# Splitting the mixers' weight chunks in two halves of two row slices each

## The reference, cut to what matters

```python
def _token_mix(xc, xl, w_in, b_in, ...):
    seg_c = _split_proj(xc @ w_in + b_in)
    seg_l = _split_proj(xl @ w_in + b_in)
    ...
    return merge(...) @ w_out

def second_block(x, ...):
    for l in range(DEPTH_2):
        x = x + 0.5 * swiglu(rmsnorm(x, ffn1_norm[l]), ...)
        h = rmsnorm(x, mix_norm[l])
        proj = h @ w_in[l]
        ...
        y = gm[:, :, 0] * (o_a @ w_branch_nsa[l]) + gm[:, :, 1] * (o_b @ w_branch_gla[l])
        x = x + y @ w_out[l]
        x = x + 0.5 * swiglu(rmsnorm(x, ffn2_norm[l]), ...)
```

## Time and profile before

| | |
|---|---|
| median of 3 runs | 2517.67 us (2512.25 to 2520.01) |
| the profiled execution | 2515.03 us, its span 2513.3 us |
| TensorE busy | 2424.2 us, 96% |
| VectorE busy | 1422.5 us, 57% |
| ScalarE busy | 1151.6 us, 46% |
| `mix_split`, L1419 | 120 instructions, 227 us on ScalarE |
| `mix_low`, L2039 | 120 instructions, 272 us on VectorE |
| mean HBM traffic | 159 GB/s |

### The profile page before, as it was taken

One profiled execution on the slowest core, in us unless ns is written; L12 is line 12 of the kernel. 1 busy time (PEld: TensorE's weight loads), 2 busy tenths in 40 slices (PEclk: granted clock), 3 DMA queues, 4 the chain that ended last, 5 costly groups with the idle time before them and its releaser, 6 DMA issues.

```text
span 2513.3 us, 33003 instructions
## 1 busy us (share of the span) xinstructions
PE 2424.2 (96%) x13542; PEld 2007.6 (80%) x13542; DVE 1422.5 (57%) x2035; ACT 1151.6 (46%) x1602; POOL 15.3 (1%) x47
## 2 busy tenths in 40 slices
PE   6999999999999989998999999999999999999998
PEld 4777788888878777887888887788888888777887
DVE  3222233746655667666666467566666654756665
ACT  4211232534532335445444468554454445864444
POOL 0000000000000000000000000000000000000000
PEclk9999999999999999999999999999999999999999
DMA  8654222323521224554454733345545545335553
GB/s 320 237 224 178 97 88 100 134 78 124 188 82 66 85 84 150 194 184 167 169 186 183 256 138 145 118 168 190 195 168 184 191 183 189 126 111 176 184 185 133
DMA packets 57653, 399.64 MB, mean 159 GB/s; under 512 B 7785, under 2 KB 8305, under 8 KB 10016
## 3 DMA queue, kind: packets, MB, share of 16 engines
q1 hardware_dynamic: 52704, 383.80, 42.1%
q10 hardware_dynamic: 3688, 9.02, 1.0%
q0 software_dynamic: 1120, 4.78, 0.5%
HBM read 396.52 MB, written 2.63 MB: 159 GB/s over the span
## 4 chain that ended last, share of the span: by engine, by line
PE 90%; DVE 5%; ACT 3%; DMA 1%; issue 1%; POOL 0%; SPq 0%; ACTq 0%; DVEq 0%
PE pair L466 82%; DMA ring<-in_stream 1%; DVE ring_parts L2039 1%; PE pair L797 1%; PE pair L592 1%; DVE ring_parts L2031 1%; PE pair L1213 1%; ACT mix_high L1419 1%; PE pair L780 1%; PE pair L1185 1%; PE pair L934 1%; PE pair L575 1%; PE pair L1199 1%; PE pair L744 0%; ACT arena L1370 0%
## 5 line engine op out<-in xcount | busy, mean ns | idle before, releaser
L466 PE MATMUL pair<-xT_parts,ring_high 128*128 128x512 f32 x2112 | 745.7, 395 | 3.3 <-DVE xT_parts L2023 3.3
L466 PE MATMUL pair<-xT_parts,ring_parts 128*128 128x256 f32 (+2 forms) x2448 | 693.9, 298 | 14.4 <-DVE ring_parts L2039 12.1
L2031 DVE TENSOR_TENSOR ring_parts<-ring,ring_high 128x2048 fp32r<-128x2048 f32 x198 | 453.6, 2292 | 160.6 <-ACT ring_high L1407 160.5
L466 PEld LDWEIGHTS pair<-xT_parts,ring_parts 128*128 128x128 f32 (+1 forms) x2448 | 460.8, 188 | 63.3 <-issue 25.4
L466 PEld LDWEIGHTS pair<-xT_parts,ring_high 128*128 128x128 f32 x2112 | 383.9, 188 | 79.2 <-issue 4.0
L1407 ACT ACTIVATE ring_high<-ring 128x2048 fp32r<-128x2048 f32 x198 | 378.1, 1911 | 97.6 <-DMA ring<-in_stream 97.4
L1451 ACT ACTIVATE arena<-pair 128x512 f32<-128x512 f32 x110 | 66.0, 600 | 309.0 <-PE pair L466 309.0
L2039 DVE TENSOR_TENSOR ring_parts<-ring,mix_high 128x2048 fp32r<-128x2048 f32 x68 | 153.5, 2286 | 67.9 <-ACT mix_high L1419 67.9
L466 PE MATMUL pair<-ring_parts,xT_parts 128*128 128x512 f32 (+1 forms) x448 | 175.7, 392 | 0.9 <-DVE rows L2247 0.9
L466 PE MATMUL pair<-mix_high,xT_parts 128*128 128x512 f32 (+1 forms) x576 | 172.9, 383 | 0.0
L466 PE MATMUL pair<-ring_parts,g_high 128*128 128x512 f32 x440 | 171.4, 390 | 0.0
(11 more groups left out here) (368 smaller groups left out, 3896.3 us busy)
## 6 DMA issues: line engine op xcount, KB each, us to landing
ring<-in_stream SPq DMA_DIRECT2D x338, 1024.0 KB, 4.8
xn<-in_mods SPq DMA_DIRECT2D x14, 1024.0 KB, 6.6
arena<-in_mods SPq DMA_DIRECT2D x14, 1024.0 KB, 9.0
arena<-in_bT ACTq DMA_DIRECT2D x1, 1536.0 KB, 10.2
bias_scratch<-bias_row POOLq DMA_DIRECT2D x1, 1536.0 KB, 9.4
X<-in_x ACTq DMA_DIRECT2D x1, 1024.0 KB, 11.9
X<-in_ctx ACTq DMA_DIRECT2D x1, 1024.0 KB, 16.4
arena<-in_bT ACTq DMA_DIRECT2D x1, 1024.0 KB, 8.2
```

The lines of the kernel that those rows point to most:

```text
L466: m = pe.matmul(o, l, r, start=start, stop=stop)
L2031: dve.tensor_tensor(out=ring_r[:, slot].rearrange("p a b -> p (a b)"), in0=w, in1=high[:, slot, :], op=ALU.subtract).then_inc(low_ready, 1)
```

## The change

The high part of a mixer chunk is made by two ScalarE copies of two slices (1024 columns) each, and the low part by two VectorE subtractions of the same size. Both count their semaphores once per half. VectorE waits before each half for that half's high part, and TensorE asks at every second slice for the half that it starts on. The ffns' chunks are left as they were. Nothing changes its place in an engine's order; every row of a mixer's split becomes two, and TensorE gets 198 more rows with a wait on `mixer_low_parts` (198 before, 396 now).

```diff
             def mix_weights(k, cols, wait):
 
                 m, slot = c.mix + k // CW, (c.chunk + k // CW) % SLOTS
-                if wait and k % CW == 0:
-                    pe.wait_ge(mix_low_ready, split_before(len(mix_chunk) - 2, m + 1))
+                if wait and k % 2 == 0:
+                    pe.wait_ge(mix_low_ready, 2 * split_before(len(mix_chunk) - 2, m) + k % CW // 2 + 1)
...
-                act.activation(mix_high(l, m), ring[:, ch % SLOTS].rearrange("p a b -> p (a b)"),
-                               ACT.Copy).then_inc(mix_high_ready, 1)
+                for half in (slice(0, 2 * N), slice(2 * N, 4 * N)):
+                    act.activation(mix_high(l, m)[:, half], ring[:, ch % SLOTS].rearrange("p a b -> p (a b)")[:, half],
+                                   ACT.Copy).then_inc(mix_high_ready, 1)
...
                 slot = (mix_chunk[l + 1] + m) % SLOTS
-                dve.wait_ge(mix_high_ready, split_before(l, m + 1))
-                w = ring[:, slot].rearrange("p a b -> p (a b)")
-                dve.tensor_tensor(out=ring_r[:, slot].rearrange("p a b -> p (a b)"), in0=w, in1=mix_high(l, m),
-                                  op=ALU.subtract).then_inc(mix_low_ready, 1)
+                for n in range(2):
+                    half = slice(2 * n * N, 2 * (n + 1) * N)
+                    dve.wait_ge(mix_high_ready, 2 * split_before(l, m) + n + 1)
+                    w = ring[:, slot].rearrange("p a b -> p (a b)")[:, half]
+                    dve.tensor_tensor(out=ring_r[:, slot].rearrange("p a b -> p (a b)")[:, half], in0=w,
+                                      in1=mix_high(l, m)[:, half], op=ALU.subtract).then_inc(mix_low_ready, 1)
```

## The result

The changed kernel took 2504.4 us, the median of 7 runs (2498.7 to 2506.7), against 2515.1 us for the kernel before, the median of 7 (2512.3 to 2520.0). The ratio of the two is 0.9946, with a 95% interval of 0.9936 to 0.9956: 0.54% faster, 13.6 us by the ratio and 10.7 by the medians.

What follows compares the result with a forecast made beforehand. TensorE, with 90% of the chain, was taken as the bound. Terms 5.6 + 1.4 + 2.3 + 0.6 - 0.4 = 9.5 us gave 2505.5 from the profile, 2508.2 from the median; predicted 2507, range 2501 to 2516.

Steps and rivals of the forecast that it cites:

- the clock: Rival: TensorE's clock drops after idle time may vanish or appear; one is about 1.7 us either way; chance 0.15.
- Price of a half: Two halves instead of a whole chunk cost ScalarE 0.08 us and VectorE 0.02 us more per chunk.
- Term 1: The two layer mixers: shorter TensorE stalls at chunks 6, 10 and 11 gain 2.8 us per layer, 5.6 in all.
- Terms 2 to 4: Gains at the norms before the layer mixers, 1.4 us; in hgrn, 2.3 us; at the end of mlstm, 0.6 us.
- Term 5: TensorE's 198 more rows with a wait cost 0 to 0.8 us, taken as 0.4.
- The ring: Rival: full DMA engines keep chunk 10's transfer from coming sooner; 1.4 of 2.8 us stay per layer, 2511; chance 0.15.
- Nothing comes through: Rival: another wait follows each shortened TensorE stall; gain 0 to 3 us, time 2516; chance 0.15.
- the bare weight loads: Rival: added TensorE waits keep 188 ns weight loads from running ahead, costing 37 us; time 2544; chance 0.05.

Runs made afterwards that it cites:

- The two comparisons: The unaltered changed kernel timed twice against the kernel before: 2504.4 against 2515.1 us, ratio 0.9946; then 2502.0 against 2517.5, ratio 0.9933.
- The first-mixers version: Against the kernel before, halves only in the mixers of mlstm and hgrn, whole chunks in the two layer mixers: 2517.3 us, ratio 1.0006.
- the two parts taken alone: Against the kernel before, halves in the two layer mixers only: 2507.5 us, ratio 0.9971; in mlstm and hgrn only: 2517.3 us, ratio 1.0006.

## Why the prediction was right

The forecast was 2507 us, faster, from a sum of 9.5 us; 2504.4 was measured, 10.7 us less by the medians and 13.6 by the ratio. The places gave what was forecast; a term that the sum left out, the clock, made up the difference.

- *Price of a half.* ScalarE's 0.95 us from start to start was right. VectorE's came out at 1.14, not 1.11, so 0.07 us a chunk instead of 0.02, and through the attention both are hidden: the changed kernel is 9.28 us ahead at 1465 us of the kernel before and 9.28 at 1800. The windows of the same stretch, of the kernel before and of the changed one:

```profile
1479.28:1579.28 100.00, 100.00 (x503) 78.71 (x502) 70.19 (x189) 79.49 (x148) 0.00 (x0) 1.00 0.37 131
```

```profile
1470.00:1570.00 100.00, 100.00 (x503) 78.71 (x502) 70.94 (x201) 80.50 (x159) 0.00 (x0) 1.00 0.37 132
```

- *Term 1.* 2.8 us per layer were forecast. The first layer gave 2.74 in the first profile and 3.03 in the third (the second has a drop at 1435.1 there). The second gave 3.98 and 4.13, of which 1.54 is clock: 2.4 to 2.6; with the slow transfer 0.5. The stalls are those forecast: 0.91 and a short one for 1.0 and 0.4 at chunk 6, 1.42 and 0.15 for 1.4 and 0.4 at chunk 11.
- *Terms 2 to 4.* Norms 0.72 each for 0.7. Chunks 41 and 42 1.67 for 1.6. The wait at the transposes fell by 0.78 for 0.7, of which 0.40 is left at their start, since a clock drop stands at 931.6 in the profile of after where it began at 935.2 before. In the second and third profiles that drop is 6.8 us long, and 10 us further on nothing is left of the 0.78. End of mlstm 0.69 for 0.6.
- *Term 5.* No row shows a cost of the added waits. From 640 to 734 us the two traces stay apart by 0.63 us to 0.02. So 0, the lower end.
- *The step that was mis-sized is the clock.* It stood among the rivals, with "one drop is about 1.7 us either way" and a chance of 0.15, and was left out of the sum. The two comparisons gave 13.6 and 16.9 us by ratio (the lower ends of their intervals are 11.1 and 13.3), 10.7 and 15.5 by medians; the places alone give 9.8 (2.74 and 2.44 for the layers, 1.44, 1.67 + 0.78, 0.69), which lies below both intervals. Three drops behind a stall, in both profiles of the kernel before and in none of the changed one, are 3.4 us, of which 3.0 go with the second norm's shorter stall in all 14 profiles. With them the sum is 13.2. That it fits so well is in part luck, for the clock takes back elsewhere: the longer drop at the transposes, one at 1435.1 (1.5 us) in the second profile, one at 1839 to 1849 in all three and in neither of the kernel before. The mean span of the three profiles is 11.3 us under the mean of the two (2504.2, 2515.6). So the clock is a term of the sum, 1 to 7 us by these figures, and no run gives it more closely.
- *The rivals.* The ring took back 1.9 us in one profile of three. In the other two the second layer's transfer took 5.25 and 5.08 us for 4.73, which is most of what separates its 0.90 and 1.04 from the forecast 1.3. (That rival's 2511 is the median less 6.7; by the rule that gave 2507 it should have been 2509.6, under the line for faster.) "Nothing comes through" and the bare weight loads are out by the rows above: the weight loads' mean is 188 ns as before.

Apart from the second norm and the chunk 6 behind it, what stays open is which clock drops a kernel gets. The first-mixers version shows that 2.75 us gained at three places can be eaten by drops elsewhere, and the two parts taken alone (7.3 less, 1.5 more) don't add up to the whole.

## What to carry to other kernels

Where one engine makes the first part of a buffer, a second the next part, and a third is waiting for both, cutting the work in halves pays by the overlap plus the early start, and costs some 0.1 us per extra instruction on an engine with time to spare; quarters add little. Count it only at the places where the third engine really waits, and then ask what stands in line behind: an instruction that waits for its input holds up all that is queued after it, and moving it takes away the wait too, not its own length alone. When differences of a few us matter, take two profiles of the same program first, and compare the starts of the same instruction place by place; the spans alone differed by up to 11 us.

## What the hardware showed that I had not expected

- The drops of the granted clock have a random part that stalls don't explain: the one at 506 us, 6.8 us long, is in four of 14 profiles (a fifth has one of 3.4 us at 507.5), in a stretch where TensorE is busy throughout, and costs 3.2 us. The kernel before ranges over 7.8 us in its first comparison and the changed one over 8.0.
- A stall of 1.76 at chunk 6 of the second layer (the version with ScalarE whole) was followed by a drop, one of 2.04 (TensorE waiting for whole chunks) was not. What goes with the drop in all 14 profiles is another one 34 us earlier, at the norm. The windows behind the two stalls, in this order, have the clock at 0.69 and at 1.00, so the length of the stall there does not decide:

```profile
2070.05:2073.45 3.40, 3.30 (x18) 3.09 (x19) 1.41 (x2) 1.48 (x1) 0.00 (x0) 0.69 1.00 424
```

```profile
2071.83:2075.23 3.40, 3.40 (x29) 3.40 (x30) 0.93 (x2) 1.71 (x2) 0.00 (x0) 1.00 1.01 426
```
- The 1 MB transfer of chunk 10 in the second layer takes 4.67 to 4.73 us in the four profiles whose ScalarE splits the layers' chunks whole, and longer in all ten with halves or quarters: 4.87 to 5.84 in seven, 6.93 to 7.16 in three of one session, in which a fourth kernel had 4.92. In the first layer chunk 10's transfer takes 4.80 to 5.16 in the 13 profiles whose chain shows it, with no such order. The cause stays open.
